# Adding the residual to the gated sample rows right after the gate, instead of later in the VectorE order

## The reference, cut to what matters

```python
def layer_output(x, gate, y_ssd, o_br, g_raw, z_a, att_norm_g, w_out):
    ...
    mix = jnp.concatenate([y_ssd, y_att], axis=-1) @ w_out
    return x + gate[:, None] * mix
...
def rms_norm(x, g):
    xf = x.astype(jnp.float32)
    y = xf * lax.rsqrt(jnp.mean(xf * xf, axis=-1, keepdims=True) + EPS)
    return y.astype(x.dtype) * g
```

## Time and profile before

| | us |
|---|---|
| median of 3 runs | 889.08 |
| lowest and highest run | 888.49, 892.44 |
| the profiled execution, its own time | 888.49 |
| its span, first to last instruction | 886.6 |
| PE busy | 827.6 (93% of the span) |
| DVE busy | 526.0 (59%) |
| ACT busy | 359.7 (41%) |
| POOL busy | 253.7 (29%) |

### The profile page before, as it was taken

The page is one execution under the profiler, slowest core; times in us unless marked ns, Lnnn a source line. Parts: engine busy times, 40 slices in busy tenths (PEclk is TensorE's granted clock), DMA queues, the critical chain, the costliest instruction groups (busy, mean ns, idle before and its releaser), DMA issues. The chain is left out here.

```text
span 886.6 us, 20081 instructions
## 1 busy us (share of the span) xinstructions
PE 827.6 (93%) x8505; PEld 541.8 (61%) x8505; DVE 526.0 (59%) x1099; ACT 359.7 (41%) x735; POOL 253.7 (29%) x212
## 2 busy tenths in 40 slices
PE   3999999999999999998999997789998999899996
PEld 2447998877788655666455546444646464654553
DVE  2146652377788645448434446886876877667711
ACT  4041002011222254555223436874765666444532
POOL 2048879350000143336111000147110130302021
PEclk8899999999999999999999998899999999999999
DMA  9952256445020100303852354601011010102021
GB/s 305 354 173 102 85 207 215 181 174 190 1 73 1 29 0 1 96 1 120 309 180 95 87 162 128 206 2 37 15 48 51 13 60 11 68 2 73 14 98 48
DMA packets 45411, 89.06 MB, mean 100 GB/s; under 512 B 4388, under 2 KB 26076, under 8 KB 43210
## 3 DMA queue, kind: packets, MB, share of 16 engines
q1 hardware_dynamic: 38202, 54.94, 19.0%
q0 software_dynamic: 6080, 31.79, 10.3%
q10 hardware_dynamic: 1040, 1.05, 0.4%
HBM read 75.49 MB, written 16.40 MB: 104 GB/s over the span
## 5 line engine op out<-in xcount | busy, mean ns | idle before, releaser
L2188 PE MATMUL PS<-W,hT 128*128 128x512 f32 x256 | 113.0, 594 | 0.3 <-DVE W L1800 0.3
L1974 DVE CUSTOM_DVE_ANT_0 PS<-PS,consts 128x640 f32<-128x640 f32 (+5 forms) x96 | 77.3, 837 | 31.5 <-PE PS L2606 31.0
L1098 POOL TENSOR_TENSOR Q<-Q,U 128x512 f32<-128x512 f32 x16 | 20.3, 1269 | 243.0 <-DVE U L2008 243.0
L2188 PEld LDWEIGHTS PS<-W,hT 128*128 128x128 f32 x256 | 47.9, 190 | 56.0 <-issue 54.8
L1412 ACT ACTIVATE hT<-PS,small 128x128 f32<-128x128 f32 (+7 forms) x64 | 47.0, 742 | 47.1 <-DVE small L1974 44.9
L2573 PE MATMUL PS<-U,Y 128*128 128x512 f32 x128 | 60.5, 605 | 0.8 <-ACT Y L1426 0.8
L2573 PE MATMUL PS<-U,Q 128*128 128x512 f32 x128 | 59.0, 599 | 0.0
L1412 ACT ACTIVATE T<-PS,small 128x640 f32<-128x640 f32 (+4 forms) x64 | 41.7, 661 | 30.4 <-DVE small L1974 30.2
L1990 DVE STREAM_TRANSPOSE hT<-hT 128x1024 f32<-128x1024 f32 (+6 forms) x29 | 42.5, 1483 | 2.0 <-ACT hT L1412 1.8
L2573 PEld LDWEIGHTS PS<-U,Q 128*128 128x128 f32 x128 | 23.5, 190 | 30.3 <-issue 30.3
L2606 PE MATMUL PS<-KTsw,W 64*128 64x512 f32 (+3 forms) x128 | 39.6, 524 | 0.8 <-ACT KcTs L1404 0.8
(11 more groups left out here) (542 smaller groups left out, 1858.4 us busy)
## 6 DMA issues: line engine op xcount, KB each, us to landing
W<-in_w_in SPq DMA_DIRECT2D x4, 2048.0 KB, 7.7
W<-in_w_ada SPq DMA_DIRECT2D x7, 1024.0 KB, 16.1
U<-in_x_prompt SPq DMA_DIRECT2D x8, 512.0 KB, 10.6
W<-in_w_ada SPq DMA_DIRECT2D x2, 2048.0 KB
U<-in_state_win_kv POOLq DMA_DIRECT2D x8, 512.0 KB
W<-in_x_prompt SPq DMA_DIRECT2D x8, 512.0 KB, 3.5
out_y_prompt<-W SPq DMA_DIRECT2D x8, 512.0 KB, 3.2
out_new_win_sample<-in_state_win_kv POOLq DMA_DIRECT2D x1, 4032.0 KB, 24.6
```

The lines of the kernel that those rows point to most:

```text
L1098: nc.gpsimd.tensor_tensor(Q3[:, i, :], Q3[:, i, :], spare, ALU.add).then_inc(s_added, 1)
L1974: ins = nc.vector.tensor_tensor_reduce(x, x, strip(u), 1.0, -NEG, ALU.add, ALU.min, sneg_m[u % 2][:, m:m + 1])
L2188: ins = nc.tensor.matmul(bank(z_bank(u)), hT3[:, k, i * P:(i + 1) * P], w, start=(k == 0), stop=(k == KT8 - 1))
```

## The change

The two additions leave the step WGATE 7 and go into RES 0, each directly behind the multiplication of the same half. In front of each stands a wait of DVE for its own multiplication (`gated` at 1, then at 2). The wait for the residual rows, `xagain[0]`, moves with them to the head of RES 0. Nothing is added or removed: 986 rows in the DVE list before and after, and the lists of PE, ACT, POOL and SP have the same rows and waits.

```diff
             for (what, u), again in zip(STEPS, AGAIN):
                 tile = MIX[u] if what in OUTPUT else None
                 r = rows(tile) if what in OUTPUT else None
-                if what == "WGATE" and u == KT8 - 1:
-                    dve.wait_ge(xagain[0], 16)
-                    dve.wait_ge(s_gated, 2)
-                    for n in range(2):
-                        x = xres[0][0:SR, n, :]
-                        nc.vector.tensor_tensor(x, x, gate_s[n], ALU.add).then_inc(s_summed, 1)
...
                     dve.wait_ge(s_out, 2 * u + again + 1)
-                    if u and again == 0:
+                    if again == 0:
                         dve.wait_ge(xagain[u % 2], 16 * (u // 2 + 1))
...
                         nc.vector.tensor_tensor(gate_s[again], use_bank("OUT", 0, 0)[SR * again:SR * again + SR], gate_s[again], ALU.mult).then_inc(s_gated, 1)
+                        dve.wait_ge(s_gated, again + 1)
+                        nc.vector.tensor_tensor(x, x, gate_s[again], ALU.add).then_inc(s_summed, 1)
```

## The result

| | before | changed |
|---|---|---|
| median, us | 891.05 (6 runs, 888.49 to 892.58) | 896.77 (6 runs, 895.68 to 897.05) |
| ratio | | 1.0064, 95% interval 1.0045 to 1.0083 |
| profiled execution, us | 888.49 | 893.61 |
| span | 886.6 | 891.7 |

The changed kernel is slower, by 5.7 us between the medians and by 5.1 us between the two profiled executions. I had forecast 890.5, between 887.0 and 893.0: the measured median lies outside. A part of the miss is in the base: with six runs the median of the kernel before is 891.05, not the 889.08 of the first three.

What follows compares the result with a forecast made beforehand. PE, busy 93% of the span, was taken as the bound. Additions at RES 0 cost 1.4 us, WGATE 7, the moved wait and early loads 0, clock as before: 889.08 + 1.4 = 890.5 us, range 887.0 to 893.0.

Steps and rivals of the forecast that it cites:

- the other working: At RES 0, addition 0 blocked until GpSimd's WGATE 0 ends, then run: 588.47 + 0.68 = 589.15.
- The row of 69.07: Earlier DVE instruction, two SBUF inputs, meeting GpSimd: took 2.41 us, ended 0.54 past GpSimd's; used to size RES 0's additions.
- The zero at WGATE 7: At WGATE 7, the 1.2 us of removed additions become DVE idle time before BACK 4: 0 on the path.
- the zero for the early loads: SP's 12 value loads issue at about 591.7 instead of 612.7, with room in the traffic: cost 0.
- 4.15 - 1.4: DVE 4.15 us late at SOFTMAX 12, against PE 1.4 us late at BACK 3.
- The 1.4 us for PE: Behind RES 0, PE waits at S 14 and starts BACK 3 at 594.92 instead of 593.52; chance 0.42.
- The rival of no cost: Third rival: at RES 0 GpSimd holds the additions up less or not at all; 889.1 us, chance 0.15.
- the term for the clock: Additional clock drop after PE's new 2.27 us idle time before S 14: 1.7 us more; chance 0.22.
- my first rival: Clock falls additionally after the new idle time before S 14: 890.5 + 1.7 = 892.2 us; chance 0.22.
- theory D: From the experiments: PE's new idle time brings low clock stretches; third round 3 to 5 us over, mean clock 0.981 to 0.983.
- The long drop of the second rival: Idle times from PV 3 to PV 4 join into one long low clock stretch: 3.4 us more, 893.9; chance 0.06.
- The faster rival: Fourth rival: idle time before S 14 removes the 1.77 "issue" idle before 599.74 and its low clock: 887.0 us; chance 0.12.

Runs made afterwards that it cites:

- a1_gpsimd_waits: Changed kernel, with GpSimd's WGATE 0 waiting for both additions instead of for OUT 0; median 893.03 us, ratio 0.9997 to the kernel before.
- a3_busy_gap: Changed kernel with 16 extra PE transposes of a constant behind PV 3, filling PE's idle time; median 897.20 us, ratio 1.0044 to the kernel before.
- z0_before: Kernel before, unaltered, profiled a second time; median 892.07 us, ratio 0.9996.
- a0_again: Changed kernel, unaltered, profiled and timed a second time; median 895.27 us in 12 runs, ratio 1.0036 to the kernel before.
- b1_six_turns: Kernel before, additions left at WGATE 7, plus six VectorE block transposes behind the multiplications of RES 0; median 896.22 us, ratio 1.0033.
- r_six_turns: Repeat of the kernel before with six VectorE block transposes behind the multiplications of RES 0; ratio 1.0020.
- c1_wgate4_waits: Kernel before with GpSimd's WGATE 4 waiting for the subtraction of SOFTMAX 17; median 893.88 us, ratio 1.0033.
- b3_eighteen_turns: Kernel before with eighteen VectorE block transposes behind the multiplications of RES 0; median 904.59 us, ratio 1.0153.

## Why the prediction was wrong

**The local mechanism held, step by step.** Addition 0 was to end at 589.01 (589.15 by the other working) and ended at 589.05; addition 1 at 591.69, measured 591.81; SOFTMAX 12 at 591.6 (0.1 before the end of its own addition 1, a slip), measured 591.84; PE's idle time 2.27, measured 2.24; BACK 3 at 594.92, measured 595.15. The row of 69.07 was the right one to size the meeting by, and a1_gpsimd_waits shows that the meeting is the cause. The zero at WGATE 7 held (idle 1.29 to 2.45), and so did the zero for the early loads. The point below which lateness is free follows from the working as 4.15 - 1.4, some 2.7 us, and is near 3. The 1.4 us for PE were right as the direct part: 1.6 at BACK 3 between the first two profiles, and 1.3 to 1.5 at BACK 4 where profiles of equal clock are set side by side. The rival of no cost is refuted. (Where the bounds call a gain the third rival, the fourth is meant.)

**What failed is the step from there to the total**: "From here all engines are 1.4 us late together", with the clock term at nothing in the sum. In the two profiles the changed kernel was 1.6 us late at BACK 3, 2.4 at BACK 4 and 5.1 at the end. Three terms of the sum and the range were at fault. First, "the median of the three runs is 0.59 above the profiled execution, and I give the changed kernel the same". The profiled execution and the first three runs lay at the low end: the median of six is 891.05, 2.0 us higher, and the 126 later runs have a mean of 891.7. With that base alone the forecast would have been 892.5 and its upper end 895, still below the 896.77 measured.

Second, "as wide as the scatter of single runs asks for (888.49 to 892.44)". The scatter of single runs of the kernel before has a standard deviation of 2.8 us. Three runs can't show that. The two profiles of the kernel before say where it sits: 0.9 us between RES 0 and BACK 4, 4.3 us behind BACK 4, and the first multiplication itself starts between 585.3 and 593.3 in profiles whose code is the same up to there. I had one of these profiles and took its stretches as fixed.

Third, the term for the clock, priced at 1.7 and left out of the sum with a chance of 0.22. In the 78 runs with SOFTMAX 12 more than 4 us late the total is 2.7 +- 0.5 us higher than in the kernel before, 1.3 more than the direct 1.4, and the mean clock is 0.0024 +- 0.0007 lower. By the 126 runs of the kernel before, that much clock goes with 1.1 us. The mean clock is not itself a price of time. From 16 to 27 us, where the DMA share was 1.09, the clock was low in the kernel before and not in the changed one:

```profile
16.00:27.00 11.00, 8.70 (x22) 0.53 1.09 358
```

```profile
16.00:27.00 11.00, 8.18 (x23) 1.00 1.09 358
```

The first row is the kernel before, the second the changed one, and both started RES 0 at the same time, 586.02 and 586.04. So the size of 2.7 is fitted by 1.4 and 1.1, and lies nearer to my first rival (1.4 + 1.7) than to my forecast. That the lower clock follows from the longer idle times of PE is not shown. The last two rounds of the changed kernel had a mean clock of 0.985, against the expectations of theory D. In the 32 us behind the first multiplication, by their mean clocks, the eight profiles of these three kernels lost 1.9 us on average, and the seven with SOFTMAX 12 at most 3 us late 1.2, with 0 to 3.4 in either group. And a3_busy_gap didn't settle it. The long drop of the second rival is an accurate description of the first profile after (clock 0.89, 3.4 us lost), but z0_before has the same, so it is no mark of the change.

**What stays open.** The first measurement says 5.7 us (ratio 1.0045 to 1.0083), the later rounds 3.1 +- 0.6 for the same kernel. The difference of 2.6 can be put down to two draws, though not to a cause. The six runs of the changed kernel there had a mean clock of 0.980, where the 31 later ones had 0.983, and their mean was 1.7 us higher (896.5 against 894.8); 0.0036 of clock go with 1.7 us. The six of the kernel before had a mean of 890.8, 0.9 below the 126. Whether the low clock of those six runs was chance I can't say. In the later rounds direct part and clock give about 2.5 of the 2.7, and whether the clock part belongs to the change at all stays open. What the runs do show is where the later rounds' whole 3.1 comes from: it is gone when only the meeting with GpSimd is taken away (0.1 +- 0.5 over the kernel before in 35 runs), and six transposes, which make VectorE late without the meeting, bring 2.2 +- 0.8.

The faster rival is gone: the "issue" idle of 1.77 did not vanish behind the new idle time in any profile. It was 1.76 to 2.04 in eight of them and 1.27 to 1.49 in a0_again, b1_six_turns and r_six_turns.

## What to carry to other kernels

Before moving a small VectorE instruction with two SBUF inputs forward, see what GpSimd does at the new place: here 0.68 us became 2.0 to 2.3, and an instruction between two such meetings waits too. Letting the GpSimd instruction wait for the short one cost nothing measurable (ratios 0.9992 to 1.0009) where GpSimd had slack. Holding GpSimd up in another place moved the meeting elsewhere and won nothing (c1_wgate4_waits). And when a mechanism is worth 1 or 2 us in 890, take the base and the width from many runs of the kernel before: a sum that is right to 0.2 us in its place can still miss the total by 6.

## What the hardware showed beyond that

- What the low stretches of the clock take comes in steps. The mean clock of the 32 us behind the first multiplication was 1.00, 0.95, 0.89, 0.84 or, with eighteen transposes, 0.73 in the seventeen profiles, so 0, 1.7, 3.4, 5.1 or 8.6 us lost. One program can show different steps: the kernel before had 0.95 once and 0.89 once, the changed kernel 1.00, 0.95 and 0.89.
- VectorE's addition 0 does not wait for both queued GpSimd instructions: it ended at 589.05, while the pair ended at 591.26. The pair took 5.11 us instead of 4.67, so GpSimd lost 0.44 us there. WGATE 2 to 7, beside which the subtraction of SOFTMAX 17 took its 2.29 us in the kernel before, lost less: 14.08 us, 2.35 each, where the undisturbed pair took 2.34 each.
- Block transposes of one SBUF tile run beside GpSimd unhindered: 0.73 us each in b1_six_turns, from 592.16 on, and 0.74 each for the eighteen of b3_eighteen_turns, most of which had no GpSimd instruction beside them.
